# Norms between stages done by token halves, a third weight buffer for each stage's first unit, and no warm-up products

## The reference, cut to what matters

```python
def rms_norm(x, g):
    y = x * lax.rsqrt(jnp.mean(x * x, axis=-1, keepdims=True) + EPS)
    return y * g

# first block, layer 0 (short convolution), layer 1 (dilated attention)
y = mixer(rms_norm(h, mix_norm_pre))
h = h + rms_norm(y, mix_norm_post)                     # transitions 1 and 3
f = swiglu(rms_norm(h, ffn_norm_pre), w_gate_up, w_down)
h = h + rms_norm(f, ffn_norm_post)                     # transitions 2 and 4
# second block (sliding-window attention beside a wide convolution), then swiglu again
h = h + rms_norm(mixed, mix_post_g)                    # transition 5
h = h + rms_norm(ff, ffn_post_g)                       # transition 6, the output
```

## Time and profile before

| | |
|---|---|
| median of three runs | 2197.34 us |
| the profiled execution's own time | 2198.08 us |
| its span, first to last instruction | 2195.9 us |
| PE busy | 2096.7 us, 95% |
| DVE busy | 1179.0 us, 54% |
| ACT busy | 707.8 us, 32% |
| mean granted TensorE clock | 0.983 of 2.4 GHz |

### The profile page before, as it was taken

How to read it: one execution, slowest core, us unless ns; L and a number is a source line. 1 busy time by engine, 2 the same in 40 slices (tenths; PEclk the granted TensorE clock), 3 DMA queues, 4 the chain that set the end, 5 groups by cost and what they waited for, 6 DMA issues and landing times.

```text
span 2195.9 us, 25960 instructions
## 1 busy us (share of the span) xinstructions
PE 2096.7 (95%) x10181; PEld 1724.3 (79%) x10181; DVE 1179.0 (54%) x1975; ACT 707.8 (32%) x1040; POOL 9.7 (0%) x23
## 2 busy tenths in 40 slices
PE   7999999999999999999997999999998799999997
PEld 5887888888788797787876788888786577888885
DVE  5646544422775757747555844432489656444324
ACT  4224322211523323333233522221343554222212
POOL 0000000000000000000000000000000000000000
PEclk9999999999999999999988999999999899999998
DMA  4762222222124151141411222232222112222221
GB/s 166 112 109 77 96 96 96 96 96 96 60 98 131 58 148 64 58 134 58 135 39 39 77 96 96 96 104 98 96 86 77 39 61 94 96 96 96 99 101 49
DMA packets 35914, 198.53 MB, mean 90 GB/s; under 512 B 3912, under 2 KB 4457, under 8 KB 14457
## 3 DMA queue, kind: packets, MB, share of 16 engines
q1 hardware_dynamic: 28248, 182.13, 23.8%
q10 hardware_dynamic: 6656, 12.58, 2.7%
q0 software_dynamic: 928, 2.70, 2.5%
HBM read 181.14 MB, written 3.67 MB: 84 GB/s over the span
## 4 chain that ended last, share of the span: by engine, by line
PE 85%; DVE 8%; ACT 4%; issue 2%; DMA 0%; SPq 0%; DVEq 0%; ACTq 0%
PE bank L1373 78%; PE bank L1596 2%; ACT w_hi L474 2%; DVE c L1249 2%; PE bank L1558 1%; PE bank L1574 1%; DVE w_lo L804 1%; DVE w_lo L802 1%; DVE p L1100 0%; DVE work L857 0%; DVE h L862 0%; ACT p L600 0%; PE bank L1746 0%; DVE v1s L1071 0%; DVE work L878 0%
## 5 line engine op out<-in xcount | busy, mean ns | idle before, releaser
L1373 PE MATMUL bank<-x_hi,w_hi 128*128 128x512 f32 x1760 | 700.7, 398 | 19.5 <-DVE x_lo L815 15.9
L1373 PE MATMUL bank<-x_hi,w_lo 128*128 128x512 f32 x1760 | 687.7, 391 | 0.0
L1373 PE MATMUL bank<-x_lo,w_hi 128*128 128x512 f32 x1760 | 687.2, 390 | 0.0
L802 DVE TENSOR_TENSOR w_lo<-w_raw,w_hi 128x2048 fp32r<-128x2048 f32 x131 | 299.7, 2291 | 469.6 <-ACT w_hi L474 469.6
L1373 PEld LDWEIGHTS bank<-x_hi,w_hi 128*128 128x128 f32 x1760 | 331.6, 188 | 101.1 <-issue 29.7
L1373 PEld LDWEIGHTS bank<-x_hi,w_lo 128*128 128x128 f32 x1760 | 331.5, 188 | 70.8
L1373 PEld LDWEIGHTS bank<-x_lo,w_hi 128*128 128x128 f32 x1760 | 331.9, 189 | 67.1 <-issue 1.4
L474 ACT ACTIVATE w_hi<-w_raw 128x2048 fp32r<-128x2048 f32 x131 | 249.8, 1907 | 375.8 <-PE bank L1373 375.8
L1373 PE MATMUL bank<-ff_hi,w_hi 128*128 (+1 forms) x528 | 205.8, 390 | 4.1 <-DVE work L878 4.1
L1373 PE MATMUL bank<-ff_hi,w_lo 128*128 (+1 forms) x528 | 205.4, 389 | 0.0
L1373 PE MATMUL bank<-ff_lo,w_hi 128*128 (+1 forms) x528 | 205.4, 389 | 0.0
(11 more groups left out here) (189 smaller groups left out, 2055.8 us busy)
## 6 DMA issues: line engine op xcount, KB each, us to landing
w_raw<-w_all SPq DMA_DIRECT2D x167, 1024.0 KB, 4.9
qk<-qk_next ACTq DMA_DIRECT2D x32, 384.0 KB, 10.6
w_raw<-w_all SPq DMA_DIRECT2D x8, 256.0 KB, 6.4
h<-x_t SPq DMA_DIRECT2D x4, 512.0 KB, 7.2
out_t<-h SPq DMA_DIRECT2D x8, 256.0 KB, 2.0
skew<-erow POOLq DMA_DIRECT2D x8, 192.0 KB, 8.7
bias<-skew POOLq DMA_DIRECT2D x8, 128.0 KB, 3.4
pos_i<-pos SPq DMA_DIRECT2D x1, 256.0 KB
```

The costliest lines, as they stand in the source:

```text
L802: ins = v.tensor_tensor(w_lo[p][:, part], w_raw[p][:, part], hi, ALU.subtract)
L1373: ins = mm(out, b if flip else a, a if flip else b, start=start and n == 0, stop=stop and n == 2, **kw)
```

## The change

It has five parts.

1. `last_rows` runs the last unit twice, for tokens 0 to 255 and then for tokens 256 to 511, with 48 products of 256 columns each time. The statistics product of the first half (`y_stat(t, 0)`) stands behind the second bank of the second half, and that of the second half (`y_stat(t, 1)`) behind the fourth block of the next stage.
2. The whole transition runs by halves of 256 tokens: copies, squares, sums, `rstd`, `residual`, `x_hi`, `x_lo`. The copies of the second half's `y` are made by ACT instead of DVE in transitions 1, 2, 4 and 6. `first_units` takes the first half's eight blocks for both units and then the second half's. The stage's third unit is rounded, and its rest taken, between the two halves.
3. A third pair of rounded and rest buffers (`w_hi2`, `w_lo2`) lies in space that is dead then. It holds the first unit of each stage, so that this unit is ready before the last one begins. In the attention stage its rest is taken inside the last pair's steps.
4. The 30 constant products are gone, and the table of Ln and Exp is loaded earlier.
5. `r_col` is made later, after the sixth unit of its stage, and the output leaves in sixteen transfers of half a block instead of eight.

```diff
+Y_ORDER = [None] + [list(range(KC)) if t == 5 else [4, 5, 6, 7, 0, 1, 2, 3] for t in range(1, 7)]
+Y_PARTS = (3, 5)
+def slot(u):
+    stages = sum(u >= last + 2 for last in LAST_ROWS[1:])
+    return 2 if u - 1 in LAST_ROWS[1:] else (u + stages) % 2
...
+            def transition(t):                      # ACT
+                last = LAST_ROWS[t]
+                if t < 6:
+                    round_unit(last + 2)
                 for m in range(KC):
+                    y_square(t, 0, m)
+                for m in range(3):
+                    y_square(t, 1, m)
+                y_rstd(t, 0)
+                for m in range(3, KC):
+                    y_square(t, 1, m)
+                    if t < 6:
+                        x_half(t, 0, m - 3)
+                if t < 6:
+                    x_half(t, 0, 5)
+                y_rstd(t, 1)
+                if t < 6:
+                    for m in (6, 7):
+                        x_half(t, 0, m)
+                    round_unit(last + 3)
+                    for m in range(KC):
+                        x_half(t, 1, m)
+                    x_rstd(t)
...
             def transition(t):                      # DVE
-                post_norm(t)
+                if t < 6:
+                    rest_unit(LAST_ROWS[t] + 2)
+                for m in range(KC):
+                    y_copy(t, 0, m)
+                    y_add(t, 0, m - 1)
+                for m in range(3):
+                    y_copy(t, 1, m)
+                    y_add(t, 1, m - 1)
                 for m in range(KC):
-                    residual(t, m)
-                    if t < 6 and m >= 2:
-                        xlo(t, m - 1)
-                        xadd(t, m - 2)
+                    residual(t, 0, m)
+                    if m + 3 < KC:
+                        y_copy(t, 1, m + 3)
+                        y_add(t, 1, m + 2)
+                    if t < 6 and m >= 1:
+                        xlo(t, m - 1, 0, tokens(0))
+                        xadd(t, m - 2, 0, tokens(0))
...
                     rest_unit(LAST_ROWS[t] + 3)
+                for m in range(KC):
+                    residual(t, 1, m)
+                    if t < 6 and m >= 1:
+                        xlo(t, m - 1, 1, tokens(1))
+                        xadd(t, m - 2, 1, tokens(1))
...
             def first_units(t, u):                  # PE
-                    for _ in range(WARM):
-                        mm(bank[1][:, 0:3 * P], ident_b[:], mask_b[:], start=True, stop=True)
-                    pe.wait_ge(w_split, u + 2)
+                pe.wait_ge(w_split, u + 2)
+                for hf in range(2):
+                    for k in range(KC):
+                        pe.wait_ge(x_ready, x_count(t, hf, k))
+                        if hf == 0 and k == 0:
+                            pe.wait_ge(y_copied[1], copied_count(t, 3))
+                        for l in range(2):
+                            for m in range(2):
+                                ins = block_of(u + l, m, banks_of(l), [k], tokens(hf))
+                        if hf == 0 and k == 3:
+                            y_stat(t, 1)
+                xstat(t)
...
             def last_rows(t, u, c, hi, lo, banks=list(range(KC)), fresh=False):
+                for hf in range(2):
+                    s = tokens(hf)
+                    for i, m in enumerate(Y_ORDER[t]):
+                        if hf:
+                            pe.wait_ge(y_copied[0], copied_count(t, i))
+                        for kk in range(2):
...
+                        if (hf, i) == (1, 1):
+                            y_stat(t, 0)
```

More of the change, by code:

```diff
@@ L300, in program @@
         y_done = sem("y_done")
-        y_copied = sem("y_copied")
+        y_copied = [sem(f"y_copied{hf}") for hf in range(2)]
         ysq_done = sem("ysq_done")
@@ L489, in rstd @@
                 nc.scalar.activation(out, out, ACT.Exp, scale=-0.5).then_inc(ready, 1)
[L491 to L503, removed]
@@ L505, in pre_norm_block, with y_square @@
-            def pre_norm_block(t, m):
+            def y_square(t, hf, i):
+                c, m = tokens(hf), Y_ORDER[t][i]
+                if hf == 0 or t in Y_PARTS:
+                    act.wait_ge(y_copied[hf], copied_count(t, i))
+                    seen = y[:, m, c]
+                else:
+                    if i < KC - 1:
+                        act.wait_ge(y_done, y_count(t, hf, i))
+                    else:
+                        act.wait_ge(unit_done, LAST_ROWS[t] + 1)
+                    seen = bank[m][:, c]
+                if i >= 3:
+                    act.wait_ge(yacc_done, yacc_count(t, hf, i - 2))
+                dst = work[:, ACC if i == 0 else 1 + i % 2, c]
+                nc.scalar.activation(dst, seen, ACT.Square).then_inc(ysq_done, 1)
+                if hf and t not in Y_PARTS:
+                    nc.scalar.activation(y[:, m, c], seen, ACT.Copy).then_inc(y_copied[1], 1)
@@ L855, in residual @@
[L855 to L870 removed]
+                    dve.wait_ge(xacc_done, xacc_count(t, hf, m - 1))
@@ new lines, in y_add, with residual @@
+            def y_add(t, hf, i):
+                if not 1 <= i <= 6:
+                    return
+                c = tokens(hf)
+                dve.wait_ge(ysq_done, ysq_count(t, hf, i))
+                if i > 1:
+                    dve.wait_ge(yacc_done, yacc_count(t, hf, i - 1))
+                v.tensor_tensor(work[:, ACC, c], work[:, ACC, c], work[:, 1 + i % 2, c], ALU.add).then_inc(yacc_done, 1)
+            def residual(t, hf, m):
+                c = tokens(hf)
+                if m == 0:
+                    dve.wait_ge(yr_ready, 2 * (t - 1) + hf + 1)
+                order.link(v.scalar_tensor_tensor(work[:, TMP + m % 2, c], y[:, m, c], gain(POST_GAIN[t] + m),
+                                                  work[:, RQ, c], ALU.mult, ALU.mult))
+                v.tensor_tensor(h[:, m, c], h[:, m, c], work[:, TMP + m % 2, c], ALU.add).then_inc(h_ready, 1)
@@ L1019, in _ @@
                     rest_unit(l + 2)
-            for l in range(2):
+            for l in range(3):
                 rest_unit(CONV_OUT + l + 2)
@@ L1511, in _ @@
             first_units(2, QKV)
-            for n in range(8):
-                cols = slice(n, S, 4) if n < 4 else slice((n - 4) * P, (n - 3) * P)
-                ins = mm(bank[2][:, n:n + 1], r_pre[0:1, cols], ones[0:1, 0:1], start=True, stop=True)
-            ins.then_inc(rcol_ps, 1)
             def v0_unit(u):
@@ L1617, in _ @@
             for lam in range(2, 6):
-                if lam == 3:
-                    pe.wait_ge(rcol_ready, 1)
                 unit(QKV + lam, lam, EV_QKV)
+            pe.wait_ge(xr_ready, 3)
+            pe.wait_ge(evac, EV_QKV + 3)
+            for n in range(8):
+                cols = slice(n, S, 4) if n < 4 else slice((n - 4) * P, (n - 3) * P)
+                ins = mm(bank[0][:, n:n + 1], r_pre[0:1, cols], ones[0:1, 0:1], start=True, stop=True)
+            ins.then_inc(rcol_ps, 1)
             pe.wait_ge(evac, EV_QKV + 4)
```

269 lines of the change are left out of this document (146 added, 123 removed).

## The result

Changed kernel: **2236.11 us** (median of 4 runs, 2234.02 to 2237.16) beside 2197.52 us before (4 runs on the same chip, 2197.18 to 2198.5). Ratio 1.0174, 95% interval [1.0156, 1.0191]: 38.6 us slower. The prediction said 2231, range 2213 to 2247, slower with 0.90. The side, the range and the mechanism hold; the terms of the clock and of the moved `r_col` were too small.

The account below looks back on a forecast made before the run. PE bounds inside stages, so only the six transitions count, where DVE already sets the pace. They sum to +23.8 us without clock falls; three falls in four, 0.75 x 14.1, make +34: 2231 us, range 2213 to 2247.

Parts of the forecast that it names:

- the clock: PE's granted clock falling behind new gaps in transitions 1 to 5: 14.1 us if all fall, three in four taken.
- the moved `r_col`: In the stage behind transition 2, moving these products later was said to take less than 1 us off.
- The walk by steps: Engine-by-engine timing of the six transitions, summing to +23.8 us without clock falls and +37.9 with all.
- pair term: Ahead of transition 3, the `FFN_B` rest in the last attention pair delays the next copy: +1.8 us.
- first stand: PE idle at the first half's statistics product inside the last unit, until ACT's copy: 3.2 us in transition 1.
- second gap: PE idle between the halves while DVE takes its rounding rest: 3.7 us in transition 1; a clock fall adds 1.1.
- a fall at a first stand: Low clock behind PE's wait at the first half's statistics slows statistics and first products: 1.4 us in transition 1.
- The rest of `FFN_B` in the last pair: DVE's rest work there stands ahead of the next copy before transition 3: 2.2 less 0.4 of slack, +1.8 us.
- The clock holds: Rival: PE's clock does not fall behind the new gaps in the transitions; 2221 us, chance 0.22.
- It costs more: Rival: every gap lowers the clock and delays in transitions 1, 3, 5 reach the fourth unit; 2235 to 2250, chance 0.17.
- Gain and loss even out: Rival: first products 3.1 us earlier, gap between halves half as long; 2195 to 2210 us, chance 0.05.
- The norms are hidden: Rival: norm work fits beside PE's products, -5.9 us in each of five transitions; 2168 us, chance 0.06.

Follow-up runs that it names:

- a3_rest: Changed kernel with DVE's rounding rest of the stage's second unit moved from between the halves to behind the second half's last sums: 2209.09 us.
- a2_stat: Changed kernel with the first half's statistics products issued behind the sixth bank of the second half instead of the second: 2227.19 us.
- a4_fill: Changed kernel with 20 constant products, results never read, in PE's gap between the halves: 2224.42 us.
- a1_rcol: Changed kernel with the 16 `r_col` products issued behind the QKV stage's third unit instead of behind the sixth: 2233.51 us.
- c1_nowarm: Kernel before with its constant products between stages left out, nothing else changed: 2205.99 us.
- c3_rest: Kernel before plus the third weight buffer, whole norms and constants kept, DVE's rest of the second unit behind the `y` copies: 2191.07 us.
- b4_fill: Changed kernel with `r_col`, first-half statistics and DVE's rest all moved later or earlier out of waits, plus 16 constant products before the first `x` column: 2199.35 us.

## Why the prediction was right

**The walk by steps held.** Per transition, predicted without and with the falls of the clock, then measured (the distance from T to the third unit or to DVE's first work, against that of before): 1: 3.6 / 6.2, measured 5.0. 2: 6.0 / 9.0, measured 9.3 at DVE's first work and 9.1 at the fourth unit, which PE waits for. 3 without its pair term: 2.0 / 4.6, measured 1.9, since the first stand did not occur there. 4: 5.5 / 8.1, measured 8.7. 5: 5.1 / 7.7, measured 7.0. 6: -0.2 / +0.5, measured -0.9 to the program's end. With 9.1 for the second these six make 30.8 for a predicted 22.0 to 36.1; with the two terms below it is 37.4 of the span's 39.4. Of what is left, some 1.3 us is the third unit itself in transitions 1, 3 and 5: the slow first product behind `xstat` (232.86 to 233.49) now belongs to it, and it takes 11.33 us for 10.88. The stands were predicted with place, releaser and size (3.2 and 3.7, measured 2.87 and 3.49), and a3_rest and a2_stat show each to be a cause.

**The clock was too small a term.** I let a fall at the second gap cost 1.1 us. a4_fill's trace has 10.8 / 5 = 2.2: in transition 1, 27 products run slowly, not 16, and DVE's pace gives nothing of it back. The 1.4 us for a fall at a first stand was right: the two stands of which a1_rcol and the changed kernel have one trace with a fall and one without give 1.4 and 1.5 at the first `x` product. With three of these the clock took some 15 us, where the forecast had 0.75 x 14.1 = 10.6. Eight of nine stands let it fall, for three in four. The total came out near in part by luck: the clock (4 us) and `r_col` (7 us, below) were too small, while the stands themselves were 0.2 to 0.3 us shorter than walked, transition 3 had only one and a short low stretch behind it, and `FFN_B` and transition 6 cost some 2 us less than priced. The constants that the change removes do end no wait, as predicted; c1_nowarm shows what they were worth all the same.

**"The moved `r_col` takes less than 1 us off" failed.** The stretch from the fourth QKV unit to the first attention group lost 6.2 us instead (14.5 to 20.7). I read the products as free in either place. In the kernel before they stood where PE was ahead of DVE's chain (behind them it still waited for `w_lo` at the fourth unit); in their new place no wait covers their 2.84 us, and the wait for `qk_next` came with them: 4.2 us in a1_rcol's trace. The remaining 2 us I had not looked at: the new wait of 4.45 us at the fourth unit leaves the clock low for 6 us, up to 3 us of product time. That part is read from the trace and no experiment took it alone.

**The rest of `FFN_B` in the last pair** was priced at +1.8 and cost 21.17 - 20.74 = +0.4 (T of transition 3 at 1220.55 against 1199.38). Even that can't be told from nothing: the same difference, M2 to T of transition 3, lies between -1.6 and +0.9 us in the other traces that have this move, with low stretches of the clock in the attention that are longer in one and shorter in another. c3_rest is 3.0 us better at M3 than at M2; 1.1 of it is its shorter stand, and there too the clock was low for less time (at the last unit of transition 3 for 3.4 us, 6.8 before).

**The rivals.** "The clock holds" (2221) is out, its falls are in the trace. "It costs more" (2235 to 2250) has the measured time in its range too, but not its mechanism: one stand of nine did not fall, and PE does not wait at the fourth units of transitions 1, 3 and 5. "Gain and loss even out" (2195 to 2210) wanted the middle gap half as long, and it is 3.49 us. "The norms are hidden" (2168) is out: it decides where my waits are too large by more than 24 us, and they were 0.2 to 0.3 us too large each.

I had put the cost of hidden norms on PE, 1.9 us per transition for its 256-column products. b4_fill, with nearly all stands gone, does not bear that out as a loss of every transition: in transition 1 its third unit comes at T + 41.7, against 43.2 in the kernel before and 42.1 in c3_rest, which has the same buffers. Still it is 8.3 us slower than c3_rest in the medians and 8.6 in the traces. Those lie elsewhere: 3.3 us from transition 2 to M2, 2.4 from transition 4 to 5, 1.2 and 1.0 in and behind transitions 3 and 5, 0.9 in the last, less 0.3 in the first. In transition 4 one cause can be read. `xstat` now stands behind both halves, and DVE's first work needs the scale `r_pre` that comes from it. PE and DVE of b4_fill, then of c3_rest:

```profile
1611.37 1.02 PE L1510 MATMUL bank<-work,ones 128*128 128x512 f32 x2
...
1613.86 1.29 DVE L980 TENSOR_TENSOR work<-bank,r_pre 128x512 f32<-128x512 f32 x2 [1.65 <-issue]
```

```profile
1604.14 1.02 PE L1419 MATMUL bank<-work,ones 128*128 128x512 f32 x2
...
1606.75 1.29 DVE L890 TENSOR_TENSOR work<-bank,r_pre 128x512 f32<-128x512 f32 x2
```

T is 1570.81 and 1567.07, so `xstat` comes at T + 40.6 for 37.1 and the first work at T + 43.1 for 39.7. DVE was idle for 1.65 us ahead of it in b4_fill (the profile names no releaser, but ACT ended `r_pre` at 1613.77, just before) and not idle in c3_rest. No run moves `xstat` alone, so how much of the difference it is stays open.

The Trainium skill's rule against this change, tiles of at least 512 elements (VectorE: DVE Perf Modes, section on the TRN2 errata), is borne out for VectorE: an addition of 256 columns takes 0.35 us from start to start (218.61 to 218.96), more than half of the 0.61 of 512.

## What to carry to other kernels

When a chain is cut in halves, ask first what work lies on the slower engine between them: here one rounding rest of 2.3 us in DVE's order opened a stand of 3.5 us that cost 5 with the clock, five times. A long wait of TensorE should be priced with the slow products behind it, and constant products in it are worth having even where they end no wait. Of a change with several parts, try the part alone that needs no cut: the third buffer gave 6 us by itself, once its rest lay in an existing wait. And look at what a cut moves to the end: here `xstat`, on whose result DVE's next work waits.

## What the runs showed of the hardware

- After a stand of 3.5 us PE's granted clock was 0.50 for 6.6 us (217.40:224.00), 0.50 again for 6 us behind one of 4.45 us (631.00:637.00), and after one of 2.87 us, ahead of which PE had been busy, it stayed at 1.00. The length of the low stretch varies: in the earlier trace rows it was 3.4 us (from 43.6 on the clock is 1.00), which I took for its length everywhere, and behind the 3.48 us gap of transition 3 it was 3.4 us again (1255.0 to 1258.3, then 1.00).
- A stand's length alone does not decide whether the clock falls. In the changed kernel it fell behind first stands of 3.54, 2.77 and 2.45 us (transitions 2, 4, 5) and not behind 2.87 (transition 1); in a1_rcol, behind the same 2.87 us in the same place, it fell. The wait of 1.79 us in transition 3 was followed by a fall in the changed kernel and by none in a3_rest (1.00 from 1221.2 to 1230.0). I have not settled what decides.
- 256-column products of TensorE follow each other every 0.120 us in the changed kernel too, 0.240 for a pair against 0.227 for one of 512.
